# Expert matrices with neighbouring rows in a partition, and another tensor order in the expert loop

## The reference, cut to what matters

```python
def hier_moe(x, wg, bg, we, be, w1, w3, w2):      # 64 experts, top-2 in one group of 8
    ...
    def expert_block(args):
        xb, e = args
        h = jax.nn.silu(xb @ w1[e]) * (xb @ w3[e])    # w1, w3: 1024 x 256
        return h @ w2[e]                              # w2: 256 x 1024
```

## Time and profile before

| | |
|---|---|
| median of the runs | 3512.41 us |
| span of the profiled execution, first to last instruction | 3520.8 us |
| that span less the median | 8.4 us |
| TensorE busy | 3118.0 us (89%) |
| MATMUL records of `up` (L1690) / of `down` (L1706) | 4096 / 8192 |
| DMA in the chain that ended last | 22% of the span |
| loads of expert matrices | 384 of 1024 KB |

### The profile page before, as it was taken

One profiled execution on the slowest core, in us unless ns is written; L12 is line 12 of the kernel. 1 busy time (PEld: TensorE's weight loads), 2 busy tenths in 40 slices (PEclk: granted clock), 3 DMA queues, 4 the chain that ended last, 5 costly groups with the idle time before them and its releaser, 6 DMA issues.

```text
span 3520.8 us, 50729 instructions
## 1 busy us (share of the span) xinstructions
PE 3118.0 (89%) x20688; PEld 2303.8 (65%) x20688; DVE 1117.5 (32%) x2151; ACT 707.7 (20%) x1262; POOL 108.7 (3%) x175
## 2 busy tenths in 40 slices
PE   4999979999799998967988888979879598888887
PEld 3888844656588886853777777544448357777773
DVE  6555422014422334433111111135674511111112
ACT  2222320123422233221000000120562210000011
POOL 0000020000000000000000000000000000000000
PEclk7999989989899999988999999989899799999999
DMA  8465322210222232210999999142000249999970
GB/s 258 156 191 174 113 83 72 72 60 1 72 96 95 90 102 64 92 48 29 366 366 367 367 366 364 62 144 72 24 1 25 72 144 366 367 367 366 366 241 24
DMA packets 451260, 590.02 MB, mean 168 GB/s; under 512 B 9264, under 2 KB 395504, under 8 KB 450912
## 3 DMA queue, kind: packets, MB, share of 16 engines
q1 hardware_dynamic: 448064, 573.38, 48.4%
q0 software_dynamic: 2288, 12.39, 1.0%
q10 hardware_dynamic: 816, 2.99, 0.3%
HBM read 586.58 MB, written 7.38 MB: 169 GB/s over the span
## 4 chain that ended last, share of the span: by engine, by line
PE 65%; DMA 22%; DVE 7%; ACT 3%; issue 2%; SPq 1%; POOLq 0%; POOL 0%; ACTq 0%; DVEq 0%
PE bank L1454 29%; DMA ring<-in_exp_w 22%; PE bank L1690 7%; PE bank L1546 6%; PE bank L1757 4%; PE bank L1674 3%; PE bank L1743 3%; PE bank L1447 2%; PE bank L1535 1%; PE bank L1443 1%; PE bank L1706 1%; SPq L421 1%; PE bank L1610 1%; ACT U L644 1%; DVE rstd L955 1%
## 5 line engine op out<-in xcount | busy, mean ns | idle before, releaser
L1454 PE MATMUL bank<-parts 128*128 128x512 f32 x3008 | 937.8, 393 | 49.7 <-DVE parts L928 49.4
L1454 PEld LDWEIGHTS bank<-parts 128*128 128x128 f32 x3008 | 567.7, 190 | 172.0 <-issue 51.1
L1454 PE MATMUL bank<-parts,ring_low 128*128 128x512 f32 x1504 | 589.1, 392 | 0.0
L1706 PE MATMUL bank<-arena,ring 128*64 128x64 f32 x8192 | 480.3, 223 | 58.9 <-ACT arena L589 58.9
L1690 PE MATMUL bank<-ring,arena 128*64 128x256 f32 x4096 | 470.5, 381 | 58.7 <-DMA ring<-in_exp_w 53.2
L1706 PEld LDWEIGHTS bank<-arena,ring 128*64 128x64 f32 x8192 | 464.4, 138 | 81.5 <-issue 44.7
L1690 PEld LDWEIGHTS bank<-ring,arena 128*64 128x64 f32 x4096 | 338.0, 137 | 152.2 <-issue 66.2
L1454 PEld LDWEIGHTS bank<-parts,ring_low 128*128 128x128 f32 x1504 | 285.1, 190 | 60.1
L922 DVE TENSOR_TENSOR ring_low<-ring,parts 128x2048 fp32r<-128x2048 f32 x96 | 215.1, 2246 | 215.2 <-ACT parts L607 214.9
L1274 DVE TENSOR_TENSOR arena<-bank,arena 128x512 f32 x128 | 88.5, 692 | 487.3 <-PE bank L1706 487.3
L710 ACT ACTIVATE arena<-bank 128x128 f32<-128x128 f32 x128 | 35.5, 277 | 1011.4 <-PE bank L1690 1011.4
(11 more groups left out here) (262 smaller groups left out, 2272.0 us busy)
## 6 DMA issues: line engine op xcount, KB each, us to landing
ring<-in_exp_w SPq DMA_DIRECT2D x384, 1024.0 KB, 11.2
ring<-in_w_ffn_in SPq DMA_DIRECT2D x44, 1024.0 KB, 6.8
ring<-in_w_ada SPq DMA_DIRECT2D x36, 1024.0 KB, 5.6
ring<-in_w_ffn_out SPq DMA_DIRECT2D x20, 1024.0 KB, 5.1
ring<-in_w_in SPq DMA_DIRECT2D x18, 1024.0 KB, 5.0
ring<-in_conv_w_in SPq DMA_DIRECT2D x12, 1024.0 KB, 5.1
ring<-in_attn_w_in SPq DMA_DIRECT2D x10, 1024.0 KB, 9.3
ring<-in_attn_w_out SPq DMA_DIRECT2D x8, 1024.0 KB, 5.1
```

The costliest lines, as they stand in the source:

```text
L1454: i = mm(o, a[:, cols[0], cols[1]], b, start=first_ and n == 0, stop=last_ and n == 2)
L1706: x = mm(bank[4 + s][r:r + 64, WIN * d:WIN * d + WIN], w[:, f, P * d + r:P * d + r + 64], HM[:, s, WIN * f:WIN * f + WIN], start=(f == 0), ...
```

## The change

All expert matrices are read with `(p k)` instead of `(k p)`: partition p holds rows 8p to 8p+7 of w1 and w3 and rows 2p and 2p+1 of w2, which are neighbours in memory, 8 KB in one piece. Product k then takes features p*8+k. For that ScalarE's evacuation in `to_tokens` writes the features of `XT` in the order (k, p), and reads its bank with a step of eight. The hidden features must be split as 2p+f, so the moving operand of `up` takes every second column. On TensorE the transposition becomes a function of its own, `turn`, ahead of the next `up`; in `down` the two halves of the output partitions alternate. ScalarE's `turned` is moved ahead of `gate_part` to match.

```diff
-                sp.dma_start(wview(slot, nk, cols), one.rearrange("a (k p) n -> p (a k) n", p=P))\
-                  .then_inc(sem(f"w_m{layer}{slot}"), 16)
+                rows = one.rearrange("a (p k) n -> p (a k) n", p=P)
+                sp.dma_start(wview(slot, nk, cols), rows).then_inc(sem(f"w_m{layer}{slot}"), 16)
...
-                    sp.dma_start(wview(slot, nk, cols), A[w][layer, slot // 3].rearrange("(k p) n -> p k n", p=P))\
-                      .then_inc(sem(f"w_m{layer}{slot}"), 16)
+                    one = A[w][layer, slot // 3]
+                    rows = one.rearrange("(p k) n -> p k n", p=P)
+                    sp.dma_start(wview(slot, nk, cols), rows).then_inc(sem(f"w_m{layer}{slot}"), 16)
...
-                    evac(XT[:, t, 512 * half:512 * half + 512], bank[g % 4][:], "xt")
+                    if n == 2:
+                        evac(XT[:, t, 512 * half:512 * half + 512], bank[g % 4][:], "xt")
+                    else:
+                        dst = XT[:, t].rearrange("p (k a) -> p k a", k=KT)[:, :, 64 * half:64 * half + 64]
+                        evac(dst, bank[g % 4][:].rearrange("p (a k) -> p k a", k=KT), "xt")
...
                 with act.Fori(1, n) as i:
+                    turned(i * 2 - 2, 0)
                     gate_part(i * 2 - 1, 1)
-                    turned(i * 2 - 2, 0)
+                    turned(i * 2 - 1, 1)
                     gate_part(i * 2, 0)
-                    turned(i * 2 - 1, 1)
                 but_last, last = ends(act)
+                turned(but_last, 0)
                 gate_part(last, 1)
-                turned(but_last, 0)
                 turned(last, 1)
...
-                            c0 = D_EXP * k + P * f
+                            c0 = D_EXP * k + f
                             x = mm(bank[s][64 * f:64 * f + 64, 0:2 * P].rearrange("p (w n) -> p w n", w=2),
-                                   XW[:, s, k], ring[:, 3 * s:3 * s + 2, c0:c0 + P],
+                                   XW[:, s, k], ring[:, 3 * s:3 * s + 2, c0:c0 + 2 * P - 1:2],
                                    start=(k == 0), stop=(k == KT - 1))
...
-                def down(e, landed16, s):
+                def turn(e, s):
                     pe.wait_ge(sem(f"moe{l}_h"), e + 1)
                     tp(bank[2 + s][:, 0:P], HB[:, s], ident).then_inc(sem(f"moe{l}_tp"), 1)
+
+                def down(e, landed16, s):
                     pe.wait_ge(sem(f"moe{l}_ht"), e + 1)
...
-                    for r in (0, 64):
-                        for d in range(KT):
-                            for f in range(2):
+                    for d in range(KT):
+                        for f in range(2):
+                            for r in (0, 64):
...
                 with pe.Fori(1, n) as i:
+                    turn(i * 2 - 2, 0)
                     up(i * 2 - 1, i * 16, 1)
                     down(i * 2 - 2, i * 16, 0)
+                    turn(i * 2 - 1, 1)
                     up(i * 2, i * 16 + 16, 0)
                     down(i * 2 - 1, i * 16, 1)
```

More of the change, by code:

```diff
@@ L1717, in moe @@
                 but_last, last = ends(pe)
+                turn(but_last, 0)
                 up(last, n * 16, 1)
                 down(but_last, n * 16, 0)
+                turn(last, 1)
                 down(last, n * 16, 1)
```

## The result

The changed kernel takes 3377.45 us (median of 4 runs, 3374.28 to 3381.14), the kernel before beside it 3512.57: ratio 0.9609, 95% interval 0.9595 to 0.9623. That is 135 us less; the forecast was 111 less, 3401, with a range of 3370 to 3450.

A forecast was written before the change was run, and what follows sets the result against it. The prediction took the expert loops to be bound by weight loads (367.6 GB/s, 8.558 us per expert). Loads -109.8, starts +5, ends -7, tokens +1 made -111 us: 3512.4 to 3401, with 3370 to 3450 holding 8 in 10.

The forecast's parts named there:

- What bounds the loop: Expert loops: loads set the pace; a faster DMA alone gives 0.4 to 0.5 us per expert, a faster TensorE alone nothing.
- Loads: Expert weights in runs of 8 KB: 410 GB/s instead of 367.6, 7.67 us per expert, 109.8 us saved in both loops.
- the signs: Expert loop's trace: 8 KB packets, 405 to 415 GB/s, expert period 7.6 to 7.8 us, and expected TensorE times and waits.
- The DMA stays fed: Steady expert loop: 7.67 us of loads queued, next issue 3.60 us later, so the queue never runs dry.
- down's order: Alternating halves in down: 2.3 us taken, bounds 1.9 and 3.76; hidden behind the loads.
- turn moved: Transposition ahead of the next up: the 0.37 us wait for ScalarE goes, 0.35 us left for the transposition.
- Step of two: Moving operand of up: taken as costing nothing; by pieces of 16 bytes up would be 3.9 us, under the loads.
- the slow case: Rival: the step of two in up costs the full 1.03 ns per column, up 7.7 us, total 3734 us; chance 0.11.
- Start of a loop: First experts: turn(0) waits behind the MEMSET, delaying up(1) and its loads; +2.5 us per layer, +5 in all.
- End of a loop: From the last up to the next stage: 9.9 us instead of 13.35, -3.5 per layer, -7 in all.
- Tokens: ScalarE's evacuations ahead of the loops: slower read with a step, +1 us in all, bounds 0 and +2 per layer.
- The clock: Rival: TensorE, less busy in the loops, drops to 1.2 GHz over a third of the experts; +98 us, chance 0.03.

The follow-up runs named there:

- e2: Changed kernel with the old layout, plain evacuation and a step of one, so only the new order on TensorE and ScalarE: 3520.62 us, ratio 1.0004 to the kernel before.
- e1: Changed kernel with the old order on TensorE and ScalarE, so only the new layout and step of two: 3463.50 us, ratio 0.9845 to the kernel before.
- e9: Changed kernel with every matrix read in two runs of 4 KB per partition (result wrong): 3401.88 us, ratio 0.9677 to the kernel before.
- e11: Changed kernel reading in the loop only 248 of 256 columns of w1 and w3, in pieces of 992 bytes: 3505.62 us, ratio 0.9970 to the kernel before.
- e3: Changed kernel with the halves of down one after the other again: 3402.94 us, ratio 0.9680 to the kernel before.
- e4: Changed kernel with the transposition back between up and down, halves still alternating: 3372.75 us, ratio 0.9592 to the kernel before.
- e7: Changed kernel with the moving operand of up at a step of one (result wrong): 3377.19 us, ratio 0.9597 to the kernel before.
- e8: Changed kernel with the moving operand of up at a step of four (result wrong): 3640.39 us, ratio 1.0348 to the kernel before.
- e6: Changed kernel with the MEMSET of YST split in two, one half before hidden(0), one behind: 3370.09 us, ratio 0.9580 to the kernel before.
- e10: Changed kernel with w1 and w3 in four runs of 2 KB per partition, w2 in two of 4 KB (result wrong): 3442.75 us, ratio 0.9788.

## Why the prediction was right, point by point

- **What bounds the loop**: right. In the changed kernel the loads do (422 GB/s, full engines), and e2 shows that TensorE's gain alone is worth nothing, e1 that the loads' gain alone ends after 56 us at TensorE. With the old order 0.42 us of slack per expert were forecast; 124 x 0.42 = 52.
- **Loads**: the mechanism was right (e9 to e11) and the term mis-sized. I took 410 GB/s, from a window of 75 packets of another queue, and made 420 the upper bound; it is 422. 195.0 MB per layer take 461.7 us and not 475.7, so the term was 138 us in place of 109.8. This is more than the whole miss of 24 us. The error lay in the 4 KB row too: 399 in a window of 1.25 us that still held packets of 1 KB; runs of 4 KB alone go at 410 (e9). For the same reason two of the signs were missed: 405 to 415 GB/s and a period of 7.6 to 7.8 us were named, 422 and 7.448 came.
- **The DMA stays fed**: right in the steady loop; not at its start, as forecast.
- **down's order**: right in kind; 1.99 us where I took 2.3, near the lower bound of 1.9. Without it the loop is 26 us longer in all (e3).
- **turn moved**: it gives nothing measurable with an alternating down (e4), and costs the 1 to 1.5 us per loop of its start. With the halves in turn it is worth 61 us: e1 and e3 differ by it alone, 3463.50 and 3402.94. So the layout needs one of the two edits to the order for most of its gain, and the alternation alone suffices: 56 us with neither, 116 with turn moved, 147 with the alternation, 143 with both.
- **Step of two**: taken as free, cost 0.18 us on up, hidden (e7). The bound for the slow case was summed a little low: 3.60 + 16 x 0.264 = 7.8 us for up, not 7.7. The reasoning by pieces of 16 bytes gave at most 3.9 us, and the measure is 3.68. That rule of the Trainium skill ("Advanced Engine Details and Errata", SBUF Cachelines), two hits on a line for full speed, agrees nearly with it: 5% off at two hits, twice the time at one (e8).
- **Start of a loop**: the mechanism was right. Between 1661 and 1665 the DMA of the changed kernel moved 0.79 MB, 199 GB/s, where 422 is its rate: some 2.1 us lost, where I had 2.5. What I missed is up(1) at the lower clock level in the second loop (e6). Of the 140.3 us of both loops the loads give 138 and the ends 8, so both starts cost 5.6 us together, against the +5 of the sum; that this sum came out so well is in part luck, as 2.6 of them are the clock's.
- **End of a loop**: 2128.31 - 2118.99 = 9.32 us from the last up, in place of 13.35: 4.0 gained, 3.5 forecast.
- **Tokens**: taken as +1. The six evacuations take 3.21 us and took 3.19: nothing.

```profile
1544.96 5.22 PE L1650 MATMUL bank<-keep,U 128*128 128x128 f32 x32 [10.35 <-ACT U L645]
...
1547.82 3.21 ACT L590 ACTIVATE arena<-bank 128x512 f32<-128x512 f32 x6 [0.26 <-PE bank L1650]
```

- **The clock**: its mean stayed at 1.00 in the steady part of both loops of the changed kernel, with waits of 1.5 us per expert. The rival was nearer than I thought. In 1700:2100 the mean is 0.90 with waits of up to 2.8 us (e2) and 2.6 (e11), 0.93 with up to 2.0 (e10, the first row), and 1.00 with up to 1.7 (e9, the second row). The rival's price was also too low: against the forecast period of 7.67 us an expert of 11 costs 3.3 more and not 2.4, so 41 of them come to 137 us, about 3540 in all.

```profile
1700.00:2100.00 400.00, 325.13 (x4848) 256.73 (x4849) 51.71 (x100) 27.64 (x100) 30.87 (x50) 0.93 1.04 394
1700.00:2100.00 400.00, 310.32 (x5044) 248.49 (x5044) 54.28 (x105) 28.82 (x104) 32.01 (x52) 1.00 1.02 410
```

## What to carry to other kernels

When two resources stand 0.4 us apart in a loop of 8.6, a faster one gives only those 0.4; look for the edit to the second before the first is priced (here 56 and 0 us alone, 135 to 143 together). Lay weights out so that what a partition takes is one run in memory, and let the contraction's order follow from that; here the permutation of features cost nothing measurable. Where a wait is moved ahead of work, look at the first pass of the loop, in which what is waited for may stand behind something long.

## What the runs showed of the hardware that I had not expected

- The rate of loads by length of run, one core: 422 GB/s at 8 KB, 410 at 4 KB, 348 at 1 KB. A cost of 9.5 ns per packet and 0.0368 ns per byte, fitted to the first and the last, gave the time with 4 and 2 KB within 4 us, and with pieces of 992 bytes 16 us too little. The 348 are from a stretch of 2 us.
- Between the step of two and that of four of an fp32 moving operand lies a cliff: 3.68 us are 5% over a step of one, 7.23 are 107%. The price doesn't grow in proportion to the step.
- Products of 64 output partitions overlap if the halves alternate, also with only 64 columns each: 31 ns per record in place of 57 to 59.
- A TensorE that waits for loads can lose its full clock (0.90 in e2, with a period of 8.57 us as before) without time lost in the steady loop, as long as the loads stay the bound; at the start of a loop the same costs time (2.6 us in the second loop of the changed kernel and in the first of e7).
